# Half-row token transposes at the head of the additions, and TensorE's program aligned once per pair of heads

## What is computed

```python
def step(s, inp):
    w_t, k_t, v_t, a_t, b_t = inp[:5]
    sa = jnp.einsum("bhvk,bhk->bhv", s, a_t)
    s = s * w_t[:, :, None, :] + sa[..., None] * b_t[:, :, None, :] + v_t[..., None] * k_t[:, :, None, :]
    y = jnp.einsum("bhvk,bhk->bhv", s, inp[5]) if emit else None
    return s, y
s, ys = lax.scan(step, s0, xs, reverse=reverse)
```

## Time and profile before

| | us |
|---|---|
| median of three runs | 2350.02 |
| lowest and highest | 2348.01, 2352.76 |
| the profiled execution, whole | 2346.09 |
| its span in the trace | 2344.2 |
| TensorE busy in the span | 2285.3 (97%) |
| the six pairs from the second to the seventh, sum | 463.42 |

### The profile page before, as it was taken

How to read it: one execution, slowest core, us unless ns; L and a number is a source line. 1 busy time by engine, 2 the same in 40 slices (tenths; PEclk the granted TensorE clock), 3 DMA queues, 4 the chain that set the end, 5 groups by cost and what they waited for, 6 DMA issues and landing times.

```text
span 2344.2 us, 60261 instructions
## 1 busy us (share of the span) xinstructions
PE 2285.3 (97%) x23364; PEld 1944.4 (83%) x23364; DVE 1223.2 (52%) x2449; ACT 1178.7 (50%) x1999; POOL 1342.1 (57%) x566
## 2 busy tenths in 40 slices
PE   6999999999999999999999999999999999999997
PEld 4787787778777888899999888888888888888886
DVE  2478778877883323466565455453444533333322
ACT  3244545454554444444444555555555555555554
POOL 1112123212332344478888878777777877778785
PEclk8999999999999999999999999999999999999999
DMA  9922112211211223267776555555555555555553
GB/s 389 381 87 66 40 60 77 66 41 58 70 65 50 81 99 108 99 222 251 256 252 244 183 166 176 168 173 173 177 172 171 181 169 172 177 177 172 170 181 134
DMA packets 101244, 360.70 MB, mean 154 GB/s; under 512 B 11184, under 2 KB 14768, under 8 KB 101072
## 3 DMA queue, kind: packets, MB, share of 16 engines
q1 hardware_dynamic: 99872, 356.89, 44.4%
q10 hardware_dynamic: 1200, 1.25, 0.2%
HBM read 356.00 MB, written 2.10 MB: 153 GB/s over the span
## 4 chain that ended last, share of the span: by engine, by line
PE 89%; DVE 2%; ACT 2%; issue 1%; DVEq 0%; ACTq 0%
PE ps L223 32%; PE ps L224 16%; PE ps L684 5%; PE ps L196 4%; PE ps L198 4%; PE ps L197 4%; PE ps L686 4%; PE ps L685 4%; PE ps L815 1%; PE ps L800 1%; PE ps L836 1%; PE ps L980 1%; PE ps L850 1%; PE ps L951 1%; PE ps L1000 1%
## 5 line engine op out<-in xcount | busy, mean ns | idle before, releaser
L187 POOL TENSOR_TENSOR wlo<-raw,whi 128x1024 fp32r<-128x1024 f32 x555 | 1336.7, 2422 | 948.7 <-ACT whi L178 898.7
L223 PE MATMUL ps<-acts,whi 128*128 128x512 f32 x3072 | 1087.6, 398 | 1.3 <-DVE acts L2794 1.3
L224 PE MATMUL ps<-acts,wlo 128*128 128x256 f32 x3072 | 856.7, 279 | 0.0
L178 ACT ACTIVATE whi<-raw 128x1024 fp32r<-128x1024 f32 x562 | 591.6, 1054 | 267.1 <-PE ps L224 138.3
L223 PEld LDWEIGHTS ps<-acts,whi 128*128 128x128 f32 x3072 | 576.2, 188 | 131.6 <-DVE acts L2794 1.6
L224 PEld LDWEIGHTS ps<-acts,wlo 128*128 128x128 f32 x3072 | 579.0, 188 | 0.9
L684 PE MATMUL ps<-acts,whi 128*128 128x512 f32 (+1 forms) x560 | 216.9, 387 | 0.9 <-DVE W L1560 0.9
L686 PE MATMUL ps<-acts,wlo 128*128 128x512 f32 (+1 forms) x560 | 190.1, 339 | 0.0
L685 PE MATMUL ps<-acts,whi 128*128 128x512 f32 (+1 forms) x560 | 189.8, 339 | 0.0
L196 PE MATMUL ps<-acts,whi 128*128 128x256 f32 (+1 forms) x576 | 181.7, 315 | 0.0
L198 PE MATMUL ps<-acts,wlo 128*128 128x256 f32 (+1 forms) x576 | 180.0, 313 | 0.0
(11 more groups left out here) (391 smaller groups left out, 3087.8 us busy)
## 6 DMA issues: line engine op xcount, KB each, us to landing
raw<-stream SPq DMA_DIRECT2D x564, 512.0 KB, 3.3
W<-stream SPq DMA_DIRECT2D x64, 512.0 KB, 9.1
graw<-stream SPq DMA_DIRECT2D x32, 512.0 KB, 4.3
W<-xT SPq DMA_DIRECT2D x4, 1024.0 KB, 8.7
XR<-xT SPq DMA_DIRECT2D x16, 128.0 KB, 5.7
outT<-XR SPq DMA_DIRECT2D x4, 512.0 KB, 3.3
cns<-consts SPq DMA_DIRECT2D x1, 928.0 KB, 11.1
cns<-consts SPq DMA_DIRECT2D x1, 896.0 KB, 7.4
```

The costliest lines, as they stand in the source:

```text
L178: nc.scalar.activation(high, raw[slot], ACT.Copy).then_inc(hi_done, 1)
L187: nc.gpsimd.tensor_tensor(wlo[slot], raw[slot], whi[slot].bitcast(F32), ALU.subtract).then_inc(lo_done, 1)
L223: nc.tensor.matmul(both_parts, whi[slot][:, k, :], hl[:, :, k0 + k, :], start=first and k == 0, stop=False)
L224: ins = nc.tensor.matmul(ps[:, bank, 0:T], wlo[slot][:, k, :], hl[:, 0, k0 + k, :], start=False, stop=last and k == UK - 1)
```

## The change

Three things change.

1. On levels two, three and four the token transposes are no longer four of 128x128 (`turned`) but eight of half the rows (`turned_tiles`): 64 partitions of the operand, a 64x64 identity, 64 columns of output. Lower halves go to bank 6, upper halves to bank 7.
2. They move. They stood between the two fills; now they stand behind both, behind `apart` and behind the wait for `xt_ev`, at the head of the additions (`grown`). ScalarE's copy on these levels (`by_token`) reads both banks, 256 columns of each, and writes runs of 64 columns. Levels one and five keep `turned`, and where they stand.
3. Once per pair, after the second group of products and two fills, `pe.addr_align(256, offset=220)` is written into TensorE's program. When the program is loaded, so many idle instructions are put in there that the next one lies 220 instructions behind the start of a block of 256. They are executed.

```diff
+            def turned_tiles(vec):
+                for t, h in itertools.product(range(4), range(2)):
+                    ins = nc.tensor.transpose(ps[:, 6 + h, C * t:C * t + C], vec[side(h), P * t:P * t + P],
+                                              ident[side(h), side(h)])
+                return ins
+
             def to_tokens(lv):
                 if lv == 1:
                     turned(BE[:, 0, :]).then_inc(R["bt_mm"].sem, 1)
                 elif lv == 2:
                     R["ev_mk"].wait(pe, i * 2 + 1)
-                    turned(BE[:, 1, :]).then_inc(R["bt_mm"].sem, 1)
+                    turned_tiles(BE[:, 1, :]).then_inc(R["bt_mm"].sem, 1)
...
             square(AL, BE, 4).then_inc(R["prod_a"].sem, 1)
             fill(2)
+            pe.addr_align(256, offset=220)
             R["ka_ok"].wait(pe, i + 1)
             R["zc"].wait(pe, i + 1)
...
                 fill(1)
-                to_tokens(lv)
                 if lv == 1:
+                    to_tokens(lv)
                     turn(lv, 1)
...
                 fill(1)
                 apart(pe)
                 R["xt_ev"].wait(pe, i * 10 + lv * 2)
+                if lv > 1:
+                    to_tokens(lv)
                 for d in range(2):
...
+            def by_token(out):
+                return nc.scalar.activation(out.rearrange("p (t h c) -> p t h c", h=2, c=C),
+                                            ps[:, 6:8, 0:T].rearrange("p h (t c) -> p t h c", c=C), ACT.Copy)
...
             def token_key(d):
                 R["kt_mm"].wait(act, i * 2 + d + 1)
-                nc.scalar.activation(tok2[:, 512 * d:512 * d + 512], ps[:, 7, :], ACT.Copy).then_inc(R["kt_ok"].sem, 1)
+                by_token(tok2[:, 512 * d:512 * d + 512]).then_inc(R["kt_ok"].sem, 1)
```

More of the change, by code:

```diff
@@ L857, in to_tokens @@
                     R["ev_mk"].wait(pe, i * 2 + 1)
-                    turned(BE[:, 1, :]).then_inc(R["bt_mm"].sem, 1)
+                    turned_tiles(BE[:, 1, :]).then_inc(R["bt_mm"].sem, 1)
                 elif lv == 3:
                     R["ev_mk"].wait(pe, i * 2 + 2)
-                    turned(KA[:, 0, :]).then_inc(R["kt_mm"].sem, 1)
+                    turned_tiles(KA[:, 0, :]).then_inc(R["kt_mm"].sem, 1)
                 elif lv == 4:
                     R["ev_q"].wait(pe, i * 2 + 1)
-                    turned(KA[:, 1, :]).then_inc(R["kt_mm"].sem, 1)
+                    turned_tiles(KA[:, 1, :]).then_inc(R["kt_mm"].sem, 1)
                 else:
@@ L1132, in turned @@
                         .then_inc(R["xt_ev"].sem, 1)
+            def by_token(out):
+                return nc.scalar.activation(out.rearrange("p (t h c) -> p t h c", h=2, c=C),
+                                            ps[:, 6:8, 0:T].rearrange("p h (t c) -> p t h c", c=C), ACT.Copy)
             def token_beta(d):
                 R["bt_mm"].wait(act, i * 2 + d + 1)
-                nc.scalar.activation(tok1[:, 512 * d:512 * d + 512], ps[:, 7, :], ACT.Copy).then_inc(R["bt_ok"].sem, 1)
+                if d:
+                    by_token(tok1[:, 512:1024]).then_inc(R["bt_ok"].sem, 1)
+                else:
+                    nc.scalar.activation(tok1[:, 0:512], ps[:, 7, :], ACT.Copy).then_inc(R["bt_ok"].sem, 1)
             def token_key(d):
                 R["kt_mm"].wait(act, i * 2 + d + 1)
-                nc.scalar.activation(tok2[:, 512 * d:512 * d + 512], ps[:, 7, :], ACT.Copy).then_inc(R["kt_ok"].sem, 1)
+                by_token(tok2[:, 512 * d:512 * d + 512]).then_inc(R["kt_ok"].sem, 1)
             if i:
```

## The result

The changed kernel is slower: 2411.36 us median of five runs (2402.42 to 2414.54) against 2351.47 (2348.01 to 2352.76), a ratio of 1.025 with a 95% interval of 1.0238 to 1.0265. The forecast was 2344.2, and the range ended at 2364. The profiled execution took 2402.42 us; its span is 56.3 us longer than that of before.

What follows compares the result with a forecast made beforehand. TensorE, busy 97% of the span, was taken as the bound, with 8.6 us of waits for its program. Transposes -1.2, alignment -4.6, idle instructions 0: 2350.0 - 5.8 = 2344.2 us, range 2338 to 2364.

Steps and rivals of the forecast that it cites:

- the weakest step: In front of each pair's head sums: 75 idle instructions, each below 20 ns, covered by queued work, cost 0 us.
- cover: At the aligned place: TensorE's queued work hides about 1.5 us of idle instructions per pair.
- turning point: At the aligned place: idle instructions cost time only from 20 ns each on.
- the upper bound: Rival, in front of the head sums: idle instructions cost 100 ns each, +48 us, 2392.2 us; chance 0.10.
- Alignment: 8.6 us of waits become 4.0: TensorE's waits for program in the pairs: 8.6 us become 0.5 in each of eight pairs, a gain of 4.6 us.
- the one: Last L836 of level two: the only block boundary without a fill in the 256 instructions ahead, waiting 0.5 us per pair.
- The rival as written: Alignment brings nothing: waits return at one place per pair, 1.0 us each; only transposes gain, 2348.8 us; chance 0.17.
- Transposes: -1.2 us: Levels two to four, first fill matmul to additions: 1.98 us in place of 2.03, 24 levels, 1.2 us gained.
- The late token copy: Rival, ScalarE's token copy: its read across two banks exceeds the slack by 0.2 us, 4.8 us lost, 2349.0; chance 0.05.
- The signs: What the trace should show: equal pairs, "issue" waits at one or two lines, no gap at L737, 1.98 us per level.
- Windows of one length: Sign: all pairs take the same time, near 75.8 us plus one wait; 2.3 or more above if idle instructions cost.

Runs made afterwards that it cites:

- the doses: Changed kernel with 11, 27, 43 or 59 idle instructions per pair in place of 75: 2355.3, 2356.6, 2369.5 and 2383.0 us.
- place 230: Changed kernel with the aligned place moved from 220 to 230 and the idle instructions jumped over: 2352.5 us, ratio 1.0002.
- e3: Changed kernel with the same alignment to 220, but TensorE jumps over the idle instructions (max_nops=0): 2353.26 us, ratio 1.001.
- place 19: Changed kernel with the aligned place moved from 220 to 19, chosen to be bad, and the idle instructions jumped over: 2365.8 us, ratio 1.0061.
- 95: Changed kernel with the aligned place moved from 220 to 95 and the idle instructions jumped over: 2352.6 us, ratio 0.9999.

## Why the prediction was wrong, point by point

*Idle instructions: 0 us, "the weakest step".* This is the step that failed, and it carries the loss: the gaps directly, the low clock as what follows from them. It had the right place, the right cover (1.5 us; the doses give 1.6) and the right turning point (20 ns; 1.6 / 75 is 21). The price was mis-sized: 74 ns where below 20 was taken. The reason given, that an idle instruction names no register and no semaphore and so is nearer to one that is passed on, confused how long an instruction lasts (13 ns, and that is short) with how soon the next may start. The rows that bore on it were those of the upper bound: two instructions of the sequencer 0.1 us apart though the first lasts 32 ns. Start to start is what a series costs, and the one pair of rows that showed a start to start was put aside as a bound. By it the sum had come to 2392, which had a chance of 0.10. The trace shows an idle instruction as the sequencer's own (NOP on PEldq, 13 ns), and that class, not the passed one, was the row to take. The 0.15 us from the sequencer to the array, taken there as an estimate, was right: in the third pair of the changed kernel the last idle instruction starts at 323.49 and the weight load of L737 at 323.64, the matmul at 323.67.

*What the step left out.* At 74 ns the sum by its own working is 2350.0 - 5.8 + 8 x (5.55 - 1.5) = 2376.6, and 35 us are missing to 2411.4; 4.6 of them are the alignment's, below. No term and no rival had the clock: it had been at 1.00 in every pair, and I never asked what it does behind a gap that no pair had had. The trace puts about 20 us on it in the profiled execution. That leaves 10 us. Much of it is a difference between executions, which no trace explains: the profiled one is the fastest of five (9 us under the median), its clock 0.983 where the other four had 0.978 to 0.981. Even the upper bound (100 ns, "2392.2") was too low, though its gaps (48 us) are longer than those measured (31.9): it had no term for the clock either.

*Alignment: 8.6 us of waits become 4.0.* The diagnosis held: the waits are TensorE waiting for its own program, at boundaries 256 instructions apart, and they move with the place. Eleven of the twelve are; the one of 1.0 us at L969 is not, so the 8.6 us hold about 1 too much. The boundaries lie where I put them, 36 instructions behind the aligned place: from the last idle instruction to the L808 that waits, the trace of the changed kernel counts 1,573 instructions in six pairs and 1,574 in the first, and 1,572 is 36 and six times 256. What was wrong is what stands there and which of them waits. The last L836 of level two, "the one" wait that I named, is 540 instructions behind the place and not 548, so the boundary falls into the fill behind it, and there was no wait. Shifted by ten (place 230) it falls on that L836, and there it waits, six times, 0.5 us in the mean, the size that I had taken. And L808 of level five, which I had called covered by the fill in the 256 instructions ahead, stands idle for 0.4 to 1.3 us in each pair: "where the 256 instructions ahead contain a fill there is no wait" is false. The gain was to be 4.6 us and is none (ratio 1.001): of the 13 crossings in a pair of `e3` (3,328 instructions) one is plainly seen, and that one costs what the scattered ones did before. The rival as written ("the waits come back, at one place in every pair, 1.0 us each") is nearly word for word what `e3` shows; its 2348.8 is 1.2 us under the kernel before, `e3` lies 2.4 above it (2353.3 against 2350.9), a difference within the spread of single runs.

*Transposes: -1.2 us.* Right: 1.98 forecast, 1.99 measured, no new wait at L784 or L793. That it was not seen as a time of its own was to be expected of 0.05%.

*The late token copy.* Did not occur: ScalarE's copy starts at 336.79 and takes 0.60 us, and TensorE waits for it nowhere.

```profile
336.79 0.60 ACT L1144 ACTIVATE W<-ps 128x512 f32<-128x512 f32 x1 [0.59 <-PE ps L855]
```

*The signs.* "A gap in front of L737 is the price of the idle instructions: 2 us refutes me" was the right test, and 3.9 us answered it. "Windows of one length" held in neither kernel: 82.4 to 85.5 after, because the low clock lasts differently long, and 76.7 to 78.6 with the branch, where the two longest hold the 1.0 us wait at L978.

## What to carry to other kernels

Price a series of instructions by the distance of their starts, never by their duration; on TensorE's sequencer here that is 74 ns for one that does nothing, against 7.4 ns for a matmul or weight load that is passed on. Ask of every new gap in TensorE's work what the clock did behind gaps of that length, and if the trace has none, carry a term for it: here it was two thirds of the gap again. Where a place in the program's blocks matters, jump over the padding (and let the jump stay within a block: into the next one, with place 19, it cost 0.7 to 1.1 us at L737), and expect that a place moves a wait for program before it removes one: here 220, 95 and 230 had theirs at L808, L776 and L836 and the same time, 2352.5 to 2353.3 us.

## What was not expected of the hardware

- Idle instructions on TensorE's sequencer last 13 ns and start 74 ns apart (75 in 5.5 us, 99 in 7.2 us). 1.6 us of them fit behind six queued fills.
- TensorE's waits for program end 1.2 to 1.7 us after the landing of a 16 KB packet, and stand at the same instruction, give or take one, in every pair that has them once the program is aligned.
- The granted clock was at 0.50 in place of 1.00 (fills 0.43 us apart rather than 0.23) at or behind all sixteen gaps of 3.9 us and more, four of eight of 2.2 to 2.9, one of 2.7 beside five of 1.6 to 1.7, and none of 0.3 to 0.7; but also behind single waits of 1.26 and 1.8 us in `e3`. In the changed kernel it fell between 2.1 us before the array's restart and 0.4 us behind it, and stayed for 3.4 to 10.2 us.
- Ten instructions of shift moved the wait for program from L808 to L836 and L684, with hardly a change in the sum of the six pairs (464.3 and 462.7 us).
- Open: why three of the eight pairs stayed at the low clock for 10.2 us and four for 3.4, with the same program and the same gap (in the three it fell 0.7 to 1.0 us before the restart, in the four between 0.6 before and 0.4 behind); why single waits of 1.3 and 1.8 us brought the clock down where gaps of 2.8 did not; and whether any of the other 252 places gives a gain.
